# Attention scores placed ahead of the turning of another pair's probabilities, with the fifth key tile's columns moved

## The reference, cut to what matters

```python
# 64-frame chunks, own chunk + 8 previous chunks, 8 heads of 64, learned relative bias
scores = jnp.einsum('bnqhd,bnkhd->bnhqk', qc, kb).astype(jnp.float32) * (HEAD_DIM_B ** -0.5) + bias[None, None]
scores = jnp.where(valid[None, :, None, None, :], scores, -jnp.inf)
p = jax.nn.softmax(scores, axis=-1).astype(v.dtype)
o = jnp.einsum('bnhqk,bnkhd->bnqhd', p, vb)
```

## Time and profile before

| | us |
|---|---|
| median of 3 runs | 1007.75 (1007.47 to 1009.31) |
| the profiled execution, its own time | 1007.23 |
| its span, first to last instruction | 1005.1 |
| PE busy in the span | 992.8 (99%) |
| DVE busy | 662.3 (66%) |
| ACT busy | 504.6 (50%) |
| POOL busy | 281.8 (28%) |

### The profile page before, as it was taken

How to read it: one execution, slowest core, us unless ns; L and a number is a source line. 1 busy time by engine, 2 the same in 40 slices (tenths; PEclk the granted TensorE clock), 3 DMA queues, 4 the chain that set the end, 5 groups by cost and what they waited for, 6 DMA issues and landing times.

```text
span 1005.1 us, 19272 instructions
## 1 busy us (share of the span) xinstructions
PE 992.8 (99%) x7460; PEld 858.9 (85%) x7460; DVE 662.3 (66%) x1262; ACT 504.6 (50%) x994; POOL 281.8 (28%) x253
## 2 busy tenths in 40 slices
PE   8999999999999999999999999999999999999997
PEld 7888888888888899999999987778888888888885
DVE  4776877757656785355555525967777777776765
ACT  5455644434444553334344326766666666666630
POOL 1457564333230042422232000022222222222200
PEclk9999999999999999999999999999999999999999
DMA  6557355365757433335544586664334443333222
GB/s 217 173 168 220 109 159 133 112 174 158 209 164 236 144 98 102 94 105 152 153 130 136 151 270 235 246 232 158 140 138 139 138 140 128 116 127 127 81 79 83
DMA packets 122857, 152.65 MB, mean 152 GB/s; under 512 B 13176, under 2 KB 75792, under 8 KB 122768
## 3 DMA queue, kind: packets, MB, share of 16 engines
q1 hardware_dynamic: 107792, 124.16, 39.2%
q10 hardware_dynamic: 14976, 27.27, 8.9%
HBM read 106.29 MB, written 48.26 MB: 154 GB/s over the span
## 4 chain that ended last, share of the span: by engine, by line
PE 94%; DMA 3%; DVE 1%; SPq 1%; ACT 1%; issue 1%; POOL 0%; DVEq 0%; ACTq 0%
PE s_ps L1859 23%; PE oo_ps L2048 16%; PE pt_ps L1859 12%; PE s_ps L1770 9%; PE oo_ps L2010 6%; PE oo_ps L1859 5%; PE s_ps L1939 5%; PE s_ps L1788 4%; PE pt_ps L1981 3%; PE pt_ps L1770 2%; PE s_ps L2048 2%; PE oo_ps L1788 2%; PE oo_ps L1824 2%; PE s_ps L1968 1%; PE pt_ps L1788 1%; DMA v_all<-st 1%
## 5 line engine op out<-in xcount | busy, mean ns | idle before, releaser
L1859 PE MATMUL s_ps<-xo_h,wf 128*128 128x288 f32 (+1 forms) x960 | 232.4, 326 | 0.0
L1859 PEld LDWEIGHTS s_ps<-xo_h,wf 128*128 128x128 f32 x960 | 163.6, 188 | 12.6 <-issue 0.2
L1859 PE MATMUL s_ps<-xo_l,wf 128*128 128x288 f32 (+1 forms) x480 | 156.5, 326 | 0.0
L1602 DVE CUSTOM_DVE_ANT_1 prob<-s_ps,bias 128x640 f32<-128x640 f32 (+1 forms) x112 | 85.8, 803 | 59.3 <-PE s_ps L1939 59.3
L1859 PE MATMUL pt_ps<-xo_h,wf 128*128 128x288 f32 (+1 forms) x480 | 119.6, 327 | 1.6 <-DVE cs L1428 1.5
L1276 ACT ACTIVATE prob<-prob,low 128x640 f32<-128x640 f32 (+3 forms) x128 | 97.4, 762 | 45.3 <-DVE low L1602 45.2
L1383 DVE TENSOR_TENSOR wf<-s,wf 128x512 fp32r<-128x512 f32 x60 | 52.9, 883 | 79.2 <-ACT wf L1075 79.2
L2048 PE MATMUL oo_ps<-wo_h,yh 128*128 128x512 f32 x248 | 100.5, 405 | 0.0
L1117 ACT ACTIVATE copy<-s_ps 128x512 f32<-128x512 f32 (+1 forms) x60 | 37.4, 623 | 122.7 <-PE s_ps L1859 122.7
L2048 PE MATMUL oo_ps<-wo_h,yl 128*128 128x512 f32 x248 | 97.0, 391 | 0.0
L2048 PE MATMUL oo_ps<-wo_l,yh 128*128 128x512 f32 x248 | 96.9, 391 | 0.0
(11 more groups left out here) (186 smaller groups left out, 2056.8 us busy)
## 6 DMA issues: line engine op xcount, KB each, us to landing
a<-w_pair ACTq DMA_DIRECT2D x80, 256.0 KB, 3.4
xt_f<-x_tiles SPq DMA_DIRECT2D x44, 256.0 KB, 3.2
r<-x SPq DMA_DIRECT2D x17, 512.0 KB, 3.6
s_k<-st SPq DMA_DIRECT2D x32, 256.0 KB, 3.7
s_q<-st SPq DMA_DIRECT2D x32, 256.0 KB, 3.0
q<-s_q SPq DMA_DIRECT2D x16, 512.0 KB, 4.2
k<-s_k SPq DMA_DIRECT2D x16, 512.0 KB, 5.1
y_out<-r SPq DMA_DIRECT2D x15, 512.0 KB, 2.6
```

The costliest lines, as they stand in the source:

```text
L1602: nc.vector.tensor_tensor_reduce(out=out, in0=src, in1=b, scale=1.0, scalar=MASKED, op0=ALU.add, op1=ALU.min, accum_out=low[:, s:s + 1]).t ...
L1859: made = nc.tensor.matmul(out, wf[:, p, side, kc, :], xx[pas][p][:, kc, c * n:(c + 1) * n], start=kc == 0 and a == 0 and p in (0, 1, 3, 5) ...
```

## The change

It exchanges neighbours in PE's order. The even block becomes `scores(2c)`, `turn(2c-2)` in every cycle. The odd block becomes `scores(2c+1)`, `turn(2c-1)` in cycles in which no stream has its scores or its turning (1 to 6 and 23 to 31; cycle 0 has no turning); in cycles 7 to 22 it stays as it was. So that scores may be written before the turning of an older unit, the fifth key tile's columns move to 896 to 1023 of `s_ps`, behind the scores' last column, still in the second bank. PE's wait for the two small copies of unit-2 leaves the middle of `scores`; in the stream cycles it now stands ahead of all of `scores(2c+1)`. DVE's `add_bias` gets two waits, for the fifth tile's copies and for the whole turning of unit-2. No instruction that computes or moves data is added or removed.

```diff
-        fifth_ps = [s_ps[half][:, 640:768] for half in range(2)]
+        fifth_ps = [s_ps[half][:, 896:1024] for half in range(2)]
...
+        def streams_in(cycle):
+            return at_cycle(cycle, 0) + at_cycle(cycle, 1)
...
+                if has_fifth(unit - 2):
+                    dve.wait_ge(pt_copied, COPIES_BEFORE[unit - 2] + h + 1)
+                if unit >= 2:
+                    dve.wait_ge(turned, TURNED_BEFORE[unit - 1])
                 dve.wait_ge(scored, 2 * unit + h + 1)
...
+                if unit % 2 and streams_in(unit // 2) and has_fifth(unit - 2):
+                    pe.wait_ge(pt_copied, COPIES_BEFORE[unit - 2] + 2)
                 for first, count, at_c in runs:
-                    if at_c == 512 and has_fifth(unit - 2):
-                        pe.wait_ge(pt_copied, COPIES_BEFORE[unit - 2] + 2)
...
             for cycle in range(CYCLES):
+                scores(2 * cycle)
                 turn(2 * cycle - 2)
-                scores(2 * cycle)
                 middle(cycle)
...
-                turn(2 * cycle - 1)
+                if streams_in(cycle):
+                    turn(2 * cycle - 1)
                 scores(2 * cycle + 1)
+                if not streams_in(cycle):
+                    turn(2 * cycle - 1)
                 weigh(2 * cycle - 2)
                 weigh(2 * cycle - 1)
```

## The result

The changed kernel took 1015.34 us (median of 4, 1013.45 to 1016.25) against 1007.61 (1007.24 to 1009.31) for the one before: a ratio of 1.0074, with a 95% interval of 1.0059 to 1.0088. The forecast was 1014.4 with a range of 1010.0 to 1018.5.

What follows compares the result with a forecast made beforehand. PE's own order was taken as the bound; -0.3 (exchange) + 4.1 (small copies) + 1.1 and 1.75 (large copy) = +6.7 us on 1007.23, 1013.9, so 1014.4 for the median, range 1010 to 1018.5.

Steps and rivals of the forecast that it cites:

- PE's order is the bound: From 604 us on PE is always busy; the change acts only through its order's length or new PE waits.
- The exchange of a block: Scores before turning in 46 blocks: 1.71 us against 1.70, -0.01 each, -0.3 us in all, bounds -2.8 and +2.8.
- Rivals 1 and 4: 1: a load hidden in each block, 1011.9, 12%; 4: shorter drain at the change of row groups, 1005.1, 8%.
- rival 2: Changeover from scores to turning costs a load, +0.06 x 46, or the DVE cover is eaten: 1017 to 1019, 9%.
- Rivals 3 and 5: 3: waits met, stream cycles cost nothing, 1010.3, 6%; 5: the change does nothing, 1007.5 to 1008, 7%.
- The wait ahead of the scores: Cycles 9 to 22: PE waits for both small copies before the first score, 0.30 or 0.29 each, 4.1 us, bounds 3.5 to 4.9.
- The cover of the large copy in cycles 23 to 31: Odd blocks without a stream: PE waits 0.12 for the large copy before weighing unit 2c-1, nine times, 1.1 us.
- Cycles 1 to 5: Same wait for the large copy with fewer key tiles: 0.35 in each of these cycles, 1.75 us.
- Cycle 6 at nothing: Left out of the large-copy cost: ACT is late anyway, PE's loads idle 0.74, later turning only uses that up.
- Edits at nothing: DVE's new waits in add_bias, with 0.5 us of cover in odd blocks, and the fifth tile's new columns cost nothing.
- Sum and sign: Slower: +6.7 us on the profiled execution's 1007.23, 1013.9; 1014.4 for the median, 0.7% more; slower at 84%.

Runs made afterwards that it cites:

- e2_odd_old: The changed kernel with the odd blocks in the old order in all cycles, the wait ahead of all scores kept in the stream cycles; 1012.2 us, 1.0054.
- e4_head_wait: The kernel before with only PE's wait for the two small copies moved ahead of the odd unit's scores in cycles 9 to 22; 1011.47 us, 1.0044.

## Why the prediction was right, point by point

**PE's order is the bound.** Right. All differences sum up along PE's order to 7.57 in the attention, and the span grew by 7.5. DVE and ACT were not busier.

**The exchange of a block, -0.01 each, -0.3 in all.** Right. The block measured 1.71 where the account said 1.71, and 1.00 of it lies ahead of the turning, as 0.11 + 0.77 + 0.12 wants it, so the step from scores to turning, which no row had shown, costs no load. In the run with the even blocks alone cycles 7 to 31 changed by -0.3 for 25 blocks; a hundredth of a microsecond a block is as fine as these starts can be read. Rivals 1 and 4 fell, and the first half of rival 2: no load and no part of the drain is saved or added. Its second half, DVE's cover eaten, came true in the early cycles alone. Rivals 3 and 5 fell with the fourteen waits. The tiling page's rule ("TensorEngine Tiling (Array Packing)", section "Key Properties", in the Trainium skill), that a change of tiling mode drains the engine, does not disagree with it: each block still has two changes, and its length stayed.

**The wait ahead of the scores, 14 x 0.30 and 0.29, 4.1.** Right in mechanism and place, small by a fifth: measured 5.00 in the changed kernel, 5.1 against the run without it. The term that was mis-sized is the release. I took 0.05 from the one case in rows 10, where the wait is the only one of its instruction and rides on it. Here other waits of the scores are written ahead of it and it is not carried, so it is 0.11; with the wait written first the loss is 3.66, below my 4.1. My upper bound for the term, 4.9, was just too low.

**The cover of the large copy in cycles 23 to 31, 9 x 0.12 = 1.1.** Right: +1.13, gone with the old order, and growing by 0.32 with a delay of the copy by 0.34.

**Cycles 1 to 5, 5 x 0.35 = 1.75.** Right in place and size: from the start of the weighings to what follows them, cycles 1, 2, 3 and 5 are longer by 0.33, 0.35, 0.36 and 0.35, and cycle 4 by 0.62. What is over in cycle 4, 0.27, is scores(10) waiting for DVE, a wait that I had not costed; 0.18 of it comes back in the block of cycle 5 (1.60 before, 1.42 after), where PE no longer waits. I had costed DVE's cover for five key tiles only (0.5 us to spare) and not for the cycles in which the weighings are still short while the bias is already 512 columns long. The waits overlap: where the second weighing waits for ACT, DVE gains that time. That is why e2_odd_old, which takes ACT's wait away, gets back 1.24 only and keeps 0.60.

**Cycle 6 at nothing.** Wrong by 0.34, and hidden by chance. In the profiled execution of the kernel before, this cycle had idle time that none of the other profiled executions has: POOL waits there for the load of the LayerNorm's offset. POOL in the kernel before, and in e4_head_wait, which is the same up to cycle 9:

```profile
660.36 0.19 POOL L1035 TENSOR_TENSOR rstd_o<-mv_o,eps 128x1 f32<-128x1 f32 x1 [26.62 <-DMA offset<-ln_b]
```

```profile
656.60 0.19 POOL L1035 TENSOR_TENSOR rstd_o<-mv_o,eps 128x1 f32<-128x1 f32 x1 [24.36 <-DMA offset<-ln_b]
```

In the second the load lands earlier, ACT's centring no longer stands in front of the large copy, and the cycle is 0.72 shorter. The runs with both blocks in the old order lie at -0.72, those with the even block alone exchanged at -0.61 to -0.63, and those with the new order in both at -0.38 to -0.40. So the change costs 0.32 to 0.34 there, as it does in its neighbours. I had read an idle time of one execution as a property of the kernel.

**Edits at nothing.** DVE's new waits cost nothing: the run with the even blocks alone has them all and is no slower. The fifth tile's new columns likewise.

**Sum and sign.** Slower, as forecast, and 0.9 above the forecast. The mis-sized release is of that size (5.0 less 4.1), though the runs scatter by more than that. One sum of the prediction does not come out: its term bounds, added up, reach from 2.2 to 11.7 over the kernel before, 1009.9 to 1019.4, and not from 1011 to 1018. The measured time lies in either range.

No run was faster than the kernel before by more than its interval. The version with the even blocks exchanged and the wait in the middle of the scores equals it (0.9999), which is as it must be where PE's order is full and the exchange is worth 0.01.

## What to carry to other kernels

On a full engine, exchanging two neighbours is worth only what the boundary between them is worth (here 0.01 of 1.7 us); look instead at what each of them covered. A product that moves from behind another takes its cover away from whatever the other had released, and a wait that moves from the middle of a step to its head gives up the half step that had hidden it. When costing a cover, go through all shapes that the loop passes, since the cover and the covered work do not shrink alike, and do not take an idle time of one profiled execution for the kernel's own.

## What the runs showed of the hardware that I had not expected

The place of a wait among several is worth 0.1 us of PE's time when it is the last to be met: 0.11 from the end of ACT's copy to the first weight load where it stands as an instruction of its own, 0.05 where the load carries it (14 waits: 5.00 against 3.66 us, which is 0.10 each: 0.06 up to the first load's start and 0.03 more up to the first product's; why the product follows its load sooner in the second case no run shows). And the pair loads of the turning, 64 rows by 128 columns, follow each other at 0.06, those of the scores with the same shape at 0.11 to 0.12.
